# Row gathers from the first two heads on, choices between row batches, and PE adding half of the value rows, in a one-core Trainium2 kernel

## The reference

```python
def peer_ffn(h, wq, subkeys, u_tab, v_tab):
    ...
    q = (hf @ wq).astype(F32).reshape(t, PEER_HEADS, 2, PEER_HALF)
    s = jnp.einsum('thpd,hpkd->thpk', q, subkeys.astype(F32))
    top_s, top_i = lax.top_k(s, PEER_TOPK)
    ...
    best_s, best_j = lax.top_k(cand_s, PEER_TOPK)
    idx = jnp.take_along_axis(cand_i, best_j, axis=-1).reshape(t, PEER_HEADS * PEER_TOPK)
    gate = jax.nn.softmax(best_s, axis=-1).reshape(t, PEER_HEADS * PEER_TOPK)
    ...
        act = jax.nn.gelu(jnp.einsum('tkd,td->tk', u_tab[ib], xb).astype(F32), approximate=False)
        return jnp.einsum('tk,tkd->td', (gb * act).astype(xb.dtype), v_tab[ib])
```

## Time and profile before

| | us |
|---|---|
| median of three runs | 3819.06 |
| lowest and highest of them | 3817.68, 3819.18 |
| span of the profiled execution | 3812.7 |
| PE busy | 2292.7 (60%) |
| DVE busy | 2474.1 (65%) |
| ACT busy | 360.6 (9%) |
| POOL busy | 1176.0 (31%) |

### The profile page before, as it was taken

The page is one execution under the profiler, slowest core; times in us unless marked ns, Lnnn a source line. Parts: engine busy times, 40 slices in busy tenths (PEclk is TensorE's granted clock), DMA queues, the critical chain, the costliest instruction groups (busy, mean ns, idle before and its releaser), DMA issues.

```text
span 3812.7 us, 32506 instructions
## 1 busy us (share of the span) xinstructions
PE 2292.7 (60%) x9670; PEld 1563.8 (41%) x9670; DVE 2474.1 (65%) x3389; ACT 360.6 (9%) x832; POOL 1176.0 (31%) x671
## 2 busy tenths in 40 slices
PE   8999999999997998997789998700000000000000
PEld 1485555557886885445678735600000000000000
DVE  0135767676994123555640014989999999999998
ACT  0122222221100000002310100100000000000000
POOL 0000111111000000000000000048888887888884
PEclk9999999999998998998899999955555555555555
DMA  9434566667443441003334433369999999999997
GB/s 369 153 122 179 216 239 228 233 229 273 148 172 133 150 147 56 23 22 114 118 114 150 180 129 114 151 255 422 422 422 422 422 422 404 422 422 422 422 422 303
DMA packets 153143, 930.65 MB, mean 244 GB/s; under 512 B 43265, under 2 KB 43554, under 8 KB 45286
## 3 DMA queue, kind: packets, MB, share of 16 engines
q0 software_dynamic: 88000, 633.51, 40.7%
q1 hardware_dynamic: 65068, 296.22, 21.5%
HBM read 902.34 MB, written 27.33 MB: 244 GB/s over the span
## 4 chain that ended last, share of the span: by engine, by line
PE 47%; DVE 17%; issue 13%; POOL 12%; DMA 8%; SPq 1%; DVEq 0%; POOLq 0%; ACT 0%; ACTq 0%
PE bank L474 18%; PE bank L535 14%; POOL arena L1686 12%; DMA arena<-peer_v_in,arena 4%; PE bank L779 3%; DVE arena L1223 3%; DVE arena L1226 3%; PE bank L451 2%; DMA arena<-peer_u_in,arena 2%; DVE arena L1568 2%; PE bank L652 1%; DVE arena L1575 1%; DMA arena<-w_ada_in 1%; PE bank L725 1%; PE bank L682 1%
## 5 line engine op out<-in xcount | busy, mean ns | idle before, releaser
L474 PE MATMUL bank<-arena 128*128 128x256 f32 x4608 | 1007.3, 380 | 30.3 <-ACT arena L919 23.4
L474 PEld LDWEIGHTS bank<-arena 128*128 128x128 f32 x4608 | 875.4, 191 | 152.0 <-issue 26.9
L1686 POOL DMA_INDIRECT arena<-peer_u_in,arena x256 | 523.9, 2046 | 881.2 <-DVE arena L1541 752.1
L1575 DVE SCALAR_TENSOR_TENSOR arena<-arena 128x2048 f32<-128x2048 f32 x256 | 602.0, 2352 | 36.6 <-DMA arena<-peer_v_in,arena 7.2
L1568 DVE CUSTOM_DVE_ANT_0 arena<-arena 128x2048 f32<-128x2048 f32 x256 | 587.1, 2293 | 44.7 <-DMA arena<-peer_u_in,arena 25.5
L1686 POOL DMA_INDIRECT arena<-peer_v_in,arena x256 | 549.2, 2145 | 99.8 <-issue 79.7
L535 PE MATMUL bank<-arena 128*128 128x512 f32 (+1 forms) x1536 | 556.3, 522 | 0.0
L535 PEld LDWEIGHTS bank<-arena 128*128 128x128 f32 x1536 | 290.7, 190 | 258.8 <-issue 241.8
L1150 DVE CUSTOM_DVE_ANT_0 arena<-arena 128x2048 f32<-128x2048 f32 x64 | 146.6, 2290 | 138.7 <-DMA arena<-w_ada_in 138.7
L1639 POOL DMA_DIRECT2D arena<-w_ada_in x64 | 34.4, 537 | 615.5 <-DVE arena L1150 422.4
L1252 DVE TENSOR_SCALAR arena<-arena 128x256 f32<-128x256 f32 (+1 forms) x48 | 16.9, 353 | 226.4 <-PE bank L615 167.7
(11 more groups left out here) (249 smaller groups left out, 2136.9 us busy)
## 6 DMA issues: line engine op xcount, KB each, us to landing
arena<-w_in_in SPq DMA_DIRECT2D x144, 1024.0 KB, 4.8
arena<-w_ada_in POOLq DMA_DIRECT2D x64, 1024.0 KB, 5.1
arena<-w_ada_in SPq DMA_DIRECT2D x16, 2048.0 KB, 10.1
arena<-w_branch_in SPq DMA_DIRECT2D x32, 1024.0 KB, 4.8
rec_scr<-arena POOLq DMA_DIRECT2D x16, 1024.0 KB, 4.9
arena<-rec_scr SPq DMA_DIRECT2D x16, 1024.0 KB, 8.6
arena<-w_out_in SPq DMA_DIRECT2D x8, 2048.0 KB, 8.8
arena<-w_q_in SPq DMA_DIRECT2D x16, 1024.0 KB, 4.8
```

The source lines that it names most:

```text
L474: m = mm(bank[b][:, 0:SEQ], wring[:, slot, k, :], src[:, k, 0:SEQ], start=(k == 0), stop=(k == KT - 1))
L1575: stt(y_acc[:, t, :], ring[:, e % 8, :], coef[:, e:e + 1], y_acc[:, t, :], ALU.mult, ALU.add).then_inc(sem("ring_used"), 1)
L1686: pool.indirect_dma_start(ring[:, e % 8, :], None, a[table], bass.IndirectOffsetOnAxis(ap=ids[:, e:e + 1].bitcast(U32), axis=0)).then_inc( ...
```

## The change

Six things change, all in the retrieval.

- The choices are made per half and pair of heads (`pick`), eight in all. The first (t = 0, heads 0 and 1) comes as soon as the first part of the scores is there. The others stand between row batches: the second between the first two dot batches, the third to the eighth each ahead of one of the next six dot batches. Each carries the softmax of its two heads.
- POOL's gathers begin after the first pick; all its instructions are written out, without loops, and it reads the row numbers where `choose` puts them (`set_idx` is gone).
- The ring has seven slots in place of eight, spread over areas that are free by then; a slot is released by the engine that used it, in the order of the rows (`row_dve`, `row_pe`).
- PE adds every second `peer_v` row (e odd) of all batches but the first: ACT writes a 128 x 128 matrix with the coefficients of 128 tokens on its diagonal (`diags`), and PE multiplies it with the row, in four products of 512 columns that accumulate in four PSUM banks per half. `residual` adds the four banks to `y_acc`.
- The dots, gelus and coefficients have two buffers; the gelu of a batch runs ahead of its use by one batch. `y_acc` lies in the weight ring, so DVE waits for the last query projection before its first add.
- The constants of the second normalisation have an area of their own and are loaded after the last query projection.

The core of the diff:

```diff
-        ring = area(HT0, 8, D)
+        ring = [area(at, D) for at in (HT0 + 4096, HT0 + 6144, R0, R0 + 2048, R0 + 16384, R0 + 18432, R0 + 26624)]
+        def on_pe(kind, t, b, e):
+            return kind == "v" and (t, b) != (0, 0) and e % 2 == 1
...
-            sp.wait_ge(sem("xn_done"), 1)
-            sp.dma_start(lnp[:, 0, :], a["ln2_g"].partition_broadcast(P)).then_inc(sem("ln2_in"), 16)
+            sp.wait_ge(sem("q_proj"), 4 + 16)
+            sp.dma_start(ln2[:, 0, :], a["ln2_g"].partition_broadcast(P)).then_inc(sem("ln2_in"), 16)
...
+            for t in range(2):
+                for b, e in pe_rows[t]:
+                    n = n_of["v", t, b] + e
+                    pe.wait_ge(sem("diag_done"), diag_at[t, b, e] + 1)
+                    pe.wait_ge(*row_in(n))
+                    for j in range(4):
+                        m = mm(bank[4 * t + j][:, :], diag[:, diag_at[t, b, e] % 8, :], ring[n % RING][:, j * N1:(j + 1) * N1],
+                               start=((b, e) == pe_rows[t][0]), stop=((b, e) == pe_rows[t][-1]))
+                    m.then_inc(sem("row_pe"), 1)
...
+            def diags(t, b):
+                act.wait_ge(sem("coef_done"), 8 * t + b + 1)
+                for e in range(TOPK):
+                    if on_pe("v", t, b, e):
+                        d = diag_at[t, b, e]
+                        if d >= 8:
+                            act.wait_ge(sem("row_pe"), d - 7)
+                        elif d == 0:
+                            act.wait_ge(sem("q_proj"), 4 + 16)
+                        af(diag[:, d % 8, :], const("ident"), ACT.Copy, scale=coef[:, b % 2, e:e + 1]).then_inc(sem("diag_done"), 1)
+
+            q_evac(0)
+            exps(0, 0)
+            q_evac(1)
+            gelus(0, 0)
+            exps(0, 1)
+            q_evac(2)
+            q_evac(3)
+            for g in range(1, 2 * PH):
+                gelus(g // PH, g % PH)
+                if g > 1:
+                    diags((g - 1) // PH, (g - 1) % PH)
+                if g < 7:
+                    exps((g + 1) // 4, (g + 1) % 4)
+                if g == PH:
                     deviation(0)
...
+            def pick(t, p):
+                dve.wait_ge(sem("sc_copied"), 1 + 4 * p + 4)
+                top16(range(4 * p, 4 * p + 4), lambda c: tv[:, t, c, :], lambda c: ti[:, t, c, :],
+                      lambda c: sc[:, t, c, :], lambda c: sc2[:, c % 4, :])
+                step(v.tensor_copy(tf[:, t, 4 * p:4 * p + 4, :], u32(ti[:, t, 4 * p:4 * p + 4, :])))
+                candidates(t, 2 * p)
+                choose(t, 2 * p)
+                dve.sem_inc(sem("idx_set"), 1)
...
+                tt(g3, b3, b3[:, :, 0:1].broadcast_to([P, 2, TOPK]), ALU.subtract).then_inc(sem("bdiff"), 1)
...
             def residual(t):
+                dve.wait_ge(sem("row_pe"), len(pe_rows[0]) + t * len(pe_rows[1]))
...
+                for j in range(4):
+                    at = slice(j * N1, (j + 1) * N1)
+                    m = tt(y_acc[:, t, at], bank[4 * t + j][:, :], y_acc[:, t, at], ALU.add)
...
+            pick(0, 0)
+            dot_batch(0, 0)
+            pick(0, 1)
+            dot_batch(0, 1)
+            make_coef(0, 0)
+            dve.wait_ge(sem("q_proj"), 4 + 16)
+            add_batch(0, 0)
+            for g in range(2, 2 * PH):
+                if g < 8:
+                    pick(g // 4, g % 4)
+                dot_batch(g // PH, g % PH)
+                make_coef((g - 1) // PH, (g - 1) % PH)
+                add_batch((g - 1) // PH, (g - 1) % PH)
+                if g == PH:
+                    residual(0)
+            make_coef(1, PH - 1)
+            add_batch(1, PH - 1)
             residual(1)
...
+            for kind, t, b in batches:
+                if kind == "u" and b % 2 == 0:
+                    pool.wait_ge(sem("idx_set"), 4 * t + b // 2 + 1)
+                for e in range(TOPK):
+                    n = n_of[kind, t, b] + e
+                    if n >= RING:
+                        who, count = used_by[n - RING]
+                        pool.wait_ge(sem(who), count)
```

More of the change, by code:

```diff
@@ L1001, in deviation, with gelus @@
                 af(rstd[:, t:t + 1], aggr[:, t, 1:2], ACT.Sqrt, bias=eps5[:, 0:1]).then_inc(sem("std_done"), 1)
[L1003 to L1012, removed]
+            def gelus(t, b):
+                act.wait_ge(sem("row_dve"), used_by[n_of["u", t, b] + TOPK - 1][1])
+                if 8 * t + b >= 2:
+                    act.wait_ge(sem("coef_done"), 8 * t + b - 1)
+                af(gelu[:, b % 2, :], dots[:, b % 2, :], ACT.Gelu).then_inc(sem("gelu_done"), 1)
+            def diags(t, b):
[22 more added lines that the diff above has]
+                if g == PH:
                     deviation(0)
[L1014 to L1015 removed]
+            diags(1, PH - 1)
             deviation(1)
@@ L1586, in _, with dot_batch @@
[L1586 to L1589, removed]
-            def residual(t):
-                dve.wait_ge(sem("ring_used"), 7 + 256 + (16 if t == 0 else 256))
+                step(tt(g3, g3, esum.unsqueeze(2).broadcast_to([P, 2, TOPK]), ALU.mult))
+            def dot_batch(t, b):
+                n = n_of["u", t, b]
+                if 8 * t + b >= 2:
+                    dve.wait_ge(sem("gelu_done"), 8 * t + b - 1)
+                for e in range(TOPK):
+                    dve.wait_ge(*row_in(n + e))
+                    if used_by[n + e][1] > 1:
+                        dve.wait_ge(sem("row_dve"), used_by[n + e][1] - 1)
+                    v.tensor_tensor_reduce(junk, ring[(n + e) % RING], h2[:, t, :], 1.0, 0.0, ALU.mult, ALU.add, dots[:, b % 2, e:e + 1]
+                                           ).then_inc(sem("row_dve"), 1)
@@ new lines, in make_coef @@
+            def make_coef(t, b):
+                if b % 2 == 0:
+                    softmax(t, b // 2)
+                dve.wait_ge(sem("gelu_done"), 8 * t + b + 1)
+                before = [d for k, d in diag_at.items() if 8 * k[0] + k[1] == 8 * t + b - 2]
+                if before:
+                    dve.wait_ge(sem("diag_done"), before[-1] + 1)
+                tt(coef[:, b % 2, :], gelu[:, b % 2, :], gate[:, t, b * TOPK:(b + 1) * TOPK], ALU.mult).then_inc(sem("coef_done"), 1)
+                dve.wait_ge(sem("coef_done"), 8 * t + b + 1)
```

176 lines of the change are left out of this document (74 added, 102 removed).

## The result

The changed kernel takes **3800.05 us** in the median of four runs (3795.80 to 3803.41), the kernel before 3819.12: a ratio of 0.9948, with a 95% interval of 0.9934 to 0.9963. That is 19 us less, where I had forecast 55. The profiled run took 3803.41 us, with a span of 3801.2. So only 2.2 us lie around the span, not the 6.4 that I had added.

What follows compares the result with a forecast made beforehand. Row stage taken as DMA bound, 2.485 us a gather. Transfers to 3681.4, plus holes 6.0, 15.1, 17.5 and 9.0, tail 25.3 and unexplained 3.8: span 3758, plus 6.4: 3764 us; range 3730 to 3805.

Steps and rivals of the forecast that it cites:

- the hole per pick: Transfer time DMA loses when a pick pauses DVE for T: 3.5 us each for picks four to eight, 17.5 together.
- pick two and the residual: DMA holes at the pick between the first dot batches, 6.0 us, and at the first half's residual, 9.0 us.
- the 3.8 us that I carried as unexplained: Remainder when the old kernel's time was rebuilt from its gathers; added unchanged to the forecast span.
- Pick three, 15.1: Pick after the first sixteen adds, all DVE's: DMA has landed all it may by 2549.4, restart 2564.5, hole 15.1 us.
- The restart: After a pause of DVE, the first dot takes 2.4 us and DMA restarts about 2.6 us after that.
- The floor and the span: First gather at 2384.8, transfers alone ending at 3681.4; measured time taken as 6.4 us above the profiled span.
- PE rows, 4.0 us at half clock: Value rows added on PE: 4.0 us each at clock 0.50, one every 4.97 us, so hidden.
- Rival A: PE rows too dear in value batches, holding POOL: slower from 6.3 us a row, 3906 us at 7.2; chance 5%.
- C: Rival: the wait for the query projection shows, PE at half clock: 19 us more, 3783 us; chance 8%.
- E: Rival: the first gather waits behind the query projection after all: 79 us more, 3843 us; chance 3%.
- B: Rival: DVE never ahead, so picks four to eight cost 16.0 us each: 62 us more, 3827 us; chance 6%.
- residual and tail: First half's residual: pause of 21.5 us. Tail at the kernel's end: 25.3 us.

Runs made afterwards that it cites:

- after: The changed kernel itself, as measured and profiled against the kernel before: 3800.05 us, ratio 0.9948.
- spread: Changed kernel with picks three to eight cut into eight pieces each, one behind each of DVE's adds of a batch: 3747.13 us.
- the kernel with all pauses gone: Spread kernel with pick two and the first half's residual also in pieces, some later picks over two add batches, PE rows in the first batch: 3727.09 us.

## Why the prediction was wrong in size

The direction, the bound and the order of the work were right; the term that failed is **the hole per pick**, T + 5.0 - 17.5 for picks four to eight: it put 3.5 us where 9.2 were lost. The forecast of 3764 can be split as the runs split the measured 3800.05:

| term | forecast | measured | from |
|---|---|---|---|
| picks three to eight | 15.1 + 17.5 = 32.6 | 58.5 | after less the kernel without these choices |
| pick two and the residual | 6.0 + 9.0 = 15.0 | 20.0 | spread less the kernel with all pauses gone (3747.13 - 3727.09), which differs in a few smaller things too |
| all else | 3716.4 | 3721.5 | the rest |

So 26 of the 36 us lie in picks three to eight, and 5 in the other two pauses.

- *Picks four to eight, 3.5 each.* The constants of the formula were matched to one pause of the trace before, the residual's, for which I read a hole of 2.4 from DMA's busy share, 0.40 of 4 us. That is too little in two ways. By bytes the same row, 109 of 422 GB/s, lost 3.0, and the 31 us behind it, at 406, another 1.2. And the store of the finished half ran inside this pause, which I had booked as a term of its own:

```profile
3198.46 0.35 SPq L432 DMA_DIRECT2D out_dram<-arena  x1
...
q1 hardware_dynamic: 144, 1.05, 41.4%
q0 software_dynamic: 78, 0.51, 20.4%
...
3206.00:3237.00 31.00, 0.00 (x0) 0.00 (x0) 30.58 (x28) 0.65 (x1) 27.04 (x14) 0.50 1.00 406
```

  The second and third line are what plain transfers and gathers moved from 3199 to 3205 (packets, MB, share of 16 engines). The store's 1.05 MB fill 2.5 us at 422 GB/s, so the gathers lost 3.0 + 1.2 + 2.5 = 6.7 us in that pause and not 2.4. (That also accounts for 1.8 of the 3.8 us that I carried as unexplained.) Carried over by the prediction's own steps (1.6 more for a T of 16.6, 2.5 more for one slot fewer, 2.5 less behind a row of PE's), 6.7 gives 8.3 for a pick; 9.2 were measured, and the last 0.9 stay open. In pick five of after, term by term: T was 16.6, not 16.0 (0.6); DMA ran dry 15.8 us after DVE's last add, not 17.5 (1.7: full to 2743.0 by the 317 GB/s); it came back at about 2750.1 (0.47 of the window), 6.3 after the pick and not 5.0 (1.3); and after that it moved less than 422 GB/s for a while, for which I had nothing (2.1). That is 5.7, from 3.5 to 9.2.
- *Pick three, 15.1*, was too high (11.8 in the windows), which hid a part of the error. With it, 5 x 9.2 + 11.8 = 57.8, close to the 58.5 of the runs. I had let DVE reach it with DMA dry already at 2549.4; in after DMA ran full to about 2563 (0.85 of the 4 us from 2560).
- *The restart.* I let DMA come back 2.6 us after the first dot. POOL's issue of the first new gather alone took 2.44 us there, against 0.94 for the gather at 2731.97. It ends at 2749.37, 0.81 after the second dot (2746.27 + 2.29 = 2748.56), and the next, from 2749.68, at 2751.81, 2.44 later, which is the step of the dots (2746.27 - 2743.82 = 2.45). It looks as if an issue did its 0.9 us only once DVE's dot is over: in the trace of after all 239 issues that start while a dot still has 0.2 us or more to run end about 0.8 us behind that dot. The Trainium skill ("SBUF — State Buffer", Who interferes with whom) says that a DVE instruction with two SBUF inputs contends with a GpSimd instruction that reads SBUF, over a port pair that is an exclusive lock. The trace agrees in these durations. The same section of the Trainium skill tells of a probe in which such a DVE instruction did not stall transfers, and no run here changed what the dots read, so the lock as the cause is argued, not shown.
- *The floor and the span.* The first gather left at 2393.42, not 2384.8. Of these 8.6 us 8.2 were there before the first pick began (2376.21 in after, 2367.99 before). The kernels above that are the same up to that point issue it between 2384.88 and 2390.45, so most of that is the spread from run to run. The other way, 6.4 us around the span were 2.2: later runs of the kernel before have time and span of the same execution, and they lie 1.6 apart, so the 6.4 seem to have held a profiled execution that was quicker than the median.
- *PE rows, 4.0 us at half clock.* The figure came out near the 3.67 measured, for a wrong reason: I took each recorded instruction for a product, where a product shows as two, so the price at half clock was about 7 us (8 x 0.867). By the four passes of the Trainium skill ("FP8 and Floating Point Precision", TensorE Precision Notes), which I weighed and set aside, a row is 4 x 4 x 512 / 2.4 GHz = 3.4 us at the full clock, as an estimate; the trace agrees with its 3.67, and "the trace differs" was wrong. What saved the term is the granted clock: in the batch shown it left 0.50 about 5 us after the first product and then stood at 1.00. The run with doubled products, at 7.1 us a row, shows about what the half clock would have cost. (Rival A's own sums turn slower than before at 6.2 us a row, not 6.3: 88x - 491 = 55.)
- *Rivals.* C did not come: PE's last projection ended at 2502.7, and DVE's first adds came after 2510. E's place was right, its price 56 us instead of 79. B came in part: the measured 9.2 us a pick lie between my 3.5 and its 16.0, but for another reason, as the slots do not cover the pause, while DVE does not want for room.
- *Right:* DMA bound at 2.485 us a gather, full wherever DVE does not pause; PE's 282 us of relief worth nothing by itself but needed as room; a hole at each pause; residual and tail within 1 us in their durations.

## What to carry to other kernels

When a queue of transfers is fed by slots that one engine frees, price each pause of that engine as its length, less what the slots cover, plus the whole restart; count the bytes lost until the rate is full again, not the busy share of the emptiest slice, and ask which transfers filled the pause from which you take the price. Work that has room on an engine is free only in pieces shorter than the cover: the same choices cost 58 us in one piece each and 6 in eight. Before moving work off an engine, ask whether the room it leaves lies where the next stall is.

## What was not expected of the hardware

A gather's issue on POOL took 0.94 us while DVE waited or ran the small steps of a choice, and 2.13 to 2.44 us beside DVE's 128x2048 dots in the lines shown; issued one dot apart, 2.45 us, gathers refill the slots after a pause no faster than DMA empties them at 2.485. And PE, which did nothing in the 52.84 us before the batch shown and stood at 0.50, was granted 0.95 from 2700 to 2704, about 5 us into it, and 1.00 from there on.
